# Latent attention with all projections first, two heads a unit, and paired row and column tiles

## What is computed

```python
def mla_project(h, w_down, q_norm_g, kv_norm_g, w_uq, w_ukv, rope):
    cq, ckv, k_rope = jnp.split(h @ w_down, [MLA_Q_RANK, MLA_Q_RANK + MLA_KV_RANK], axis=-1)   # 256, 128, 32
    q = (rms_norm(cq, q_norm_g) @ w_uq).reshape(b, s, MLA_HEADS, MLA_NOPE_DIM + MLA_ROPE_DIM)     # 16 heads, 64 + 32
    q_nope, q_rope = jnp.split(q, [MLA_NOPE_DIM], axis=-1)
    kv = (rms_norm(ckv, kv_norm_g) @ w_ukv).reshape(b, s, MLA_HEADS, MLA_NOPE_DIM + MLA_V_DIM)    # 64 + 64
    k_nope, v = jnp.split(kv, [MLA_NOPE_DIM], axis=-1)
...
def mla_attend(q_nope, q_rope, k_nope, k_rope, v):
    s = (jnp.einsum("bqhd,bkhd->bhqk", q_nope, k_nope)
         + jnp.einsum("bqhr,bkr->bhqk", q_rope, k_rope)).astype(jnp.float32) * (96 ** -0.5)
    p = jax.nn.softmax(s, axis=-1)
    return jnp.einsum("bhqk,bkhe->bqhe", p.astype(v.dtype), v)
```

## Time and profile before

| | us |
|---|---|
| median of 3 runs | 3339.03 |
| lowest, highest | 3336.78, 3340.29 |
| profiled execution | 3339.83 |
| span of its instructions | 3338.5 |
| PE busy in it | 3183.1 (95%) |

### The profile page before, as it was taken

How to read it: one execution, slowest core, us unless ns; L and a number is a source line. 1 busy time by engine, 2 the same in 40 slices (tenths; PEclk the granted TensorE clock), 3 DMA queues, 4 the chain that set the end, 5 groups by cost and what they waited for, 6 DMA issues and landing times.

```text
span 3338.5 us, 51700 instructions
## 1 busy us (share of the span) xinstructions
PE 3183.1 (95%) x21554; PEld 2698.6 (81%) x21554; DVE 1752.5 (52%) x3094; ACT 1404.9 (42%) x2364; POOL 997.9 (30%) x440
## 2 busy tenths in 40 slices
PE   5999999999999998999989999999999999999999
PEld 3777777776677776679989987877999978779999
DVE  3353333555543334666656646555456556654564
ACT  3432222444332223544444445554444446554443
POOL 0312222110212212123433332333444433434433
PEclk8999999999999999999999999999999999999999
DMA  8345544422455552125525542333545433334454
GB/s 290 122 144 164 164 158 133 135 94 89 127 176 167 174 165 90 39 64 182 193 90 164 183 131 81 103 100 98 165 143 188 154 120 99 93 101 152 152 178 151
DMA packets 469303, 460.04 MB, mean 138 GB/s; under 512 B 9040, under 2 KB 467664, under 8 KB 469072
## 3 DMA queue, kind: packets, MB, share of 16 engines
q1 hardware_dynamic: 465760, 453.32, 42.6%
q10 hardware_dynamic: 3312, 3.42, 0.3%
HBM read 455.66 MB, written 1.05 MB: 137 GB/s over the span
## 4 chain that ended last, share of the span: by engine, by line
PE 77%; DVE 13%; ACT 6%; issue 3%; DMA 1%; ACTq 0%; POOL 0%; DVEq 0%
PE bank L399 21%; PE bank L401 20%; PE bank L400 20%; ACT wh L346 3%; DVE wl L362 3%; PE bank L443 3%; DVE hl L760 1%; DVE hidl L760 1%; PE bank L1525 1%; PE bank L1516 1%; PE bank L2258 1%; PE bank L552 1%; DVE tmp L648 1%; PE bank L457 1%; PE bank L1067 1%
## 5 line engine op out<-in xcount | busy, mean ns | idle before, releaser
L374 POOL TENSOR_TENSOR wl<-raw,wh 128x768 fp32r<-128x768 f32 (+1 forms) x336 | 879.8, 2619 | 2159.7 <-ACT wh L346 2149.8
L346 ACT ACTIVATE wh<-raw 128x2048 fp32r<-128x2048 f32 x336 | 636.4, 1894 | 318.4 <-PE bank L401 308.6
L362 DVE TENSOR_TENSOR wl<-raw,wh 128x1280 fp32r<-128x1280 f32 (+1 forms) x336 | 499.6, 1487 | 419.5 <-ACT wh L346 410.6
L399 PE MATMUL bank<-nh,wh 128*128 128x272 f32 (+1 forms) x1712 | 508.1, 297 | 4.5 <-DVE nl L1843 2.8
L401 PE MATMUL bank<-nh,wl 128*128 128x272 f32 (+1 forms) x1712 | 496.1, 290 | 0.0
L400 PE MATMUL bank<-nl,wh 128*128 128x272 f32 (+1 forms) x1712 | 494.5, 289 | 0.0
L399 PE MATMUL bank<-xh,wh 128*128 128x512 f32 (+2 forms) x1264 | 443.0, 350 | 7.8 <-DVE xl L655 5.2
L400 PE MATMUL bank<-xl,wh 128*128 128x512 f32 (+2 forms) x1264 | 432.1, 342 | 0.0
L401 PE MATMUL bank<-xh,wl 128*128 128x512 f32 (+2 forms) x1264 | 431.5, 341 | 0.0
L399 PE MATMUL bank<-hh,wh 128*128 128x512 f32 (+1 forms) x1024 | 350.3, 342 | 3.7 <-DVE X L668 1.9
L399 PEld LDWEIGHTS bank<-nh,wh 128*128 128x128 f32 x1712 | 328.4, 192 | 21.2 <-issue 17.7
(11 more groups left out here) (427 smaller groups left out, 5749.2 us busy)
## 6 DMA issues: line engine op xcount, KB each, us to landing
raw<-in_mlp_w SPq DMA_DIRECT2D x128, 1024.0 KB, 5.3
raw<-in_mod_w SPq DMA_DIRECT2D x83, 1024.0 KB, 5.2
raw<-in_w_in SPq DMA_DIRECT2D x60, 1024.0 KB, 5.2
raw<-in_w_mlp_up SPq DMA_DIRECT2D x32, 1024.0 KB, 5.4
raw<-in_w_mlp_down SPq DMA_DIRECT2D x32, 1024.0 KB, 5.2
raw<-in_w_in SPq DMA_DIRECT2D x34, 512.0 KB, 4.6
raw<-in_w_ssd_down SPq DMA_DIRECT2D x16, 1024.0 KB, 5.2
early<-in_mod_w SPq DMA_DIRECT2D x13, 1024.0 KB, 12.0
```

Source lines behind the costliest of these rows:

```text
L346: nc.scalar.activation(self.wtile(self.wh, c1), self.rawtile(c1), AF.Copy).then_inc(*up("act_wh", ("wh", c1)))
L362: nc.vector.tensor_tensor(l, r, h.bitcast(F32), ALU.subtract).then_inc(*up("dve_wl", ("wl_dve", c1)))
L374: nc.gpsimd.tensor_tensor(l, r, h.bitcast(F32), ALU.subtract).then_inc(*up("pool_wl", ("wl_pool", c1)))
L399: nc.tensor.matmul(o, ah, bh, start=first, stop=False)
```

## The change

- The stream of weights is reordered: the chunk with ckv and k_rope is first, then cq, both halves of keys and values, both halves of queries. DVE's share of the split of the four middle chunks goes from 5/8 to 2/8. The raw tile of a late chunk is the one used longest ago, not number modulo three.
- The columns of w_uq and w_ukv are sorted on the host: the 64-wide parts of eight heads first, then the rotary or value parts.
- cq is computed for the 256 latent tokens alone. The roots of both norms use `dve_quarter_root`, the nine-step DVE chain of the other norms, on four column tiles of a quarter of the tokens; ACT's logarithm and exponential are gone.
- The rotary key is copied to the four groups of 32 rows by four small matmuls and rotated once on 128 rows (`mKR`, kept in tile `tmp3`).
- All keys and values (`mkn`, `mv`), then all queries (`mqn`: eight tiles of two heads; `mqr`: four tiles of four heads, four rotations) are made before the first score.
- A unit of the attention is two heads by one block of 128 queries, 16 units. The scores are two matmuls of 64 rows of contraction on different row groups (line 1571 of the kernel after) and two of 32 rows (1574), accumulated in the same two banks; units alternate between banks 0, 1 and 2, 3. Values are four pairs of 128x64 by 128 queries (1592) on two column groups, into bank 6 or 7. Division and copy are shared between ACT (1683, 1689) and DVE (1771, 1777), and there are three tiles of exponentials.
- Scores lead transposes by two units and values by three. The first six of eight row blocks of output groups 0 and 1 are put between the last units.

The core of the diff:

```diff
+            w(("down", 1), a["mla_w_down"][0], 0, 8, 256, 160)
             w(("down", 0), a["mla_w_down"][0], 0, 8, 0, 256)
-            w(("down", 1), a["mla_w_down"][0], 0, 8, 256, 160)
             for h in range(2):
-                w(("uq", h), a["mla_w_uq"][0], 0, 2, 768 * h, 768)
-                w(("ukv", h), a["mla_w_ukv"][0], 0, 1, 1024 * h, 1024)
+                w(("ukv", h), a["mla_w_ukv"][0], 0, 1, 1024 * h, 1024, 2)
+            for h in range(2):
+                w(("uq", h), a["mla_w_uq"][0], 0, 2, 768 * h, 768, 2)
             for j in range(4):
                 w(("mwo", j), a["mla_w_o"][0], 0, 8, 256 * j, 256)
...
-                t = d % 2 if self.dense[max(d - 4, 0)] < mods[-1] else d % RAWS
+                t = d % 2 if self.dense[max(d - 4, 0)] < mods[-1] else min(range(RAWS), key=lambda i: last[i])
...
+        c = self.ix["down", 0]
+        hi, lo = self.pe_take(c)
+        os = [self.pe_bank((2 + m,), "md", 2 + m)[:, LAT] for m in range(2)]
+        for k in range(8):
+            for m, o in enumerate(os):
+                cs = slice(128 * m, 128 * m + 128)
+                ins = self.mm3(o, hi[:, k, cs], lo[:, k, cs], XH[:, k, LAT], XL[:, k, LAT], k == 0, k == 7)
+                if k == 7:
+                    ins.then_inc(*up("pe_acc", ("acc", "md", 2 + m), *([("used", c)] if m else [])))
+            if k == 2:
+                self.pe_latent(0)
+        self.pe_spread("mkv", BOTH, (5,))
+        raw, turn = self.pe_bank((6,), "mkraw"), self.pe_bank((7,), "mkturn")
...
+        for i in range(4):
+            nc.tensor.matmul(raw[32 * i:32 * i + 32, :], self.ident[0:32, 0:32], self.mkr[0:32, :], start=True, stop=True)
+        for i in range(4):
+            ins = nc.tensor.matmul(turn[32 * i:32 * i + 32, LAT], self.permm[0:32, 0:32], self.mkr[0:32, LAT], start=True, stop=True)
+        ins.then_inc(*up("pe_rope", ("acc", "mkrep")))
+        self.pe_latent(1)
         for hf in range(2):
...
             c = self.ix["ukv", hf]
...
+            hi, lo = (x[:, 0, :] for x in self.pe_take(c))
+            PE.wait_ge(*at("mch", 0, 0))
+            PE.wait_ge(*at("mcl", 0, 0))
+            for p in range(4):
+                b = self.pe_bank(RING, "mk", 4 * hf + p)
+                hs = slice(128 * p, 128 * p + 128)
+                self.mm3(b[:], hi[:, hs], lo[:, hs], self.ckh[:], self.ckl[:], True, True).then_inc(*up("pe_acc", ("acc", "mk", 4 * hf + p)))
+                b = self.pe_bank(RING, "mv", hf, p)
+                tk = slice(128 * p, 128 * p + 128)
+                self.mm3(b[:], self.ckh[:, tk], self.ckl[:, tk], hi[:, 512:1024], lo[:, 512:1024], True, True
+                         ).then_inc(*up("pe_acc", ("acc", "mv", hf, p), *([("used", c)] if p == 3 else [])))
+            if hf == 0:
+                self.pe_spread("mq", LAT, (5,))
+        for i in range(12):
+            self.pe_mla_query(i)
+        for s in range(19):
+            self.pe_mla_step(s)
+            if s in (16, 17):
+                self.pe_mwo(s - 16, 0, 6)
+        for g in range(8):
+            self.pe_mwo(g, 6 if g < 2 else 0, 8)
...
+    QUERIES = (("r", 0), ("n", 0), ("n", 1), ("r", 1), ("n", 2), ("n", 3), ("r", 2), ("n", 4), ("n", 5), ("r", 3), ("n", 6), ("n", 7))
+
+    def pe_mla_query(self, i):
+
...
+        w, n = self.QUERIES[i]
+        c = self.ix["uq", i // 6]
+        hi, lo = self.pe_take(c)
...
+        b = self.pe_bank(RING, "mq", w, n)
+        for k in range(2):
+            H, L = self.mcq[k]
...
+            ins = self.mm3(b[:, LAT], hi[:, k, cs], lo[:, k, cs], H, L, k == 0, k == 1)
+        ins.then_inc(*up("pe_acc", ("acc", "mq", w, n), *([("used", c)] if i % 6 == 5 else [])))
+        if w == "n" and n % 2:
+            self.pe_rope(("m", n // 2), self.mQR[:, n // 2, :], 256, self.permm[:], (7,))
...
+    def pe_mla_step(self, s):
...
+        if s < 16:
+            p, q = s // 2, s % 2
+            qs = slice(128 * q, 128 * q + 128)
+            bs = [self.pe_bank((2 * q + i,), "ms", s, i) for i in range(2)]
+            PE.wait_ge(*at("mqn", p))
+            PE.wait_ge(*at("mkn", p))
+            PE.wait_ge(*at("turned", "m", p // 2))
+            PE.wait_ge(*at("mkturned"))
+            PE.wait_ge(*at("mkcopied"))
+            for i, b in enumerate(bs):
+                r = slice(64 * i, 64 * i + 64)
+                nc.tensor.matmul(b[:], self.mQN[r, p, qs], self.mKN[r, p, :], start=True, stop=False)
+            for i, b in enumerate(bs):
+                r = slice(32 * ((2 * p + i) % 4), 32 * ((2 * p + i) % 4) + 32)
+                nc.tensor.matmul(b[:], self.mQR[r, p // 2, qs], self.mKR[r, :], start=False, stop=True).then_inc(*up("pe_scores", ("acc", "ms", s, i)))
+        u = s - 2
+        if 0 <= u < 16:
+            for i in range(2):
+                b = self.pe_bank((4 + i,), "mt", u, i)
+                PE.wait_ge(*at("mp", u, i))
+                for t in range(4):
+                    ins = nc.tensor.transpose(b[:, 128 * t:128 * t + 128], self.mE[u % 3][:, i, 128 * t:128 * t + 128], self.ident[:])
+                ins.then_inc(*up("pe_turned", ("acc", "mt", u, i)))
+        u = s - 3
+        if 0 <= u < 16:
+            p, q = u // 2, u % 2
+            b = self.place["mo", p] if q else self.pe_bank((6 + p % 2,), "mo", p)
+            PE.wait_ge(*at("mv", p // 4, 3))
+            for i in range(2):
+                PE.wait_ge(*at("mpt", u, i))
+            for t in range(4):
+                for i in range(2):
+                    ins = nc.tensor.matmul(b[64 * i:64 * i + 64, 128 * q:128 * q + 128], self.mV[:, t, 128 * p + 64 * i:128 * p + 64 * i + 64],
+                                           self.mPT[u % 2][:, 4 * i + t, :], start=(t == 0), stop=(t == 3))
+            ins.then_inc(*up("pe_values", ("acc", "mo", u)))
...
+        for i in range(12):
+            self.act_mla_query(i)
+        self.act_split(self.ix["uq", 0])
+        self.act_split(self.ix["uq", 1])
+        for s in range(19):
+            self.act_mla_step(s)
...
+        for n in range(4):
+            self.dve_rope(("m", n), self.mQR[:, n, :], slice(0, 128), 256, cos, sin, self.tmp[n % 3])
+        self.dve_split(self.ix["uq", 0])
+        self.dve_split(self.ix["uq", 1])
+        for s in range(19):
+            self.dve_mla_step(s)
```

More of the change, by code:

```diff
@@ new lines, in pe_mla, with pe_latent @@
+        for i in range(12):
[6 more added lines that the diff above has]
+            self.pe_mwo(g, 6 if g < 2 else 0, 8)
+    def pe_latent(self, u):
+        nc, at, up, PE = self.nc, self.T.at, self.T.up, self.PE
+        keys, T, g, dim, parts = self.latent(u)
+        name = ("mkv", "mq")[u]
+        b = self.pe_bank((4,), "tot", name)
+        for n in range(len(keys)):
+            PE.wait_ge(*at("msq", u, n))
+            for rows, ts, w in self.quarters(T):
+                ins = nc.tensor.matmul(b[rows, 0:w], self.ones[:, 0:32], self.tmp[u + n][:, ts], start=(n == 0), stop=(n == len(keys) - 1))
+        ins.then_inc(*up("pe_acc", ("acc", "tot", name)))
@@ L1561, in act_mla @@
-        rs, rtt, rv = self.mroot
-        ACT.wait_ge(*at("mvar", 1))
-        nc.scalar.activation(rtt[:], rv[:], AF.Ln).then_inc(*ACT.step())
-        ACT.wait_ge(*ACT.now())
-        nc.scalar.activation(rs[:], rtt[:], AF.Exp, scale=-0.5).then_inc(*up("act_root", ("mroot",)))
-        for k in range(3):
-            H = self.cqh[:, k, :] if k < 2 else self.ckh[:]
-            ACT.wait_ge(*at("mct", k))
-            nc.scalar.activation(H, self.tmp[k][:], AF.Copy).then_inc(*up("act_mch", ("mch", k)))
@@ new lines, in act_mla @@
+        for hf in range(2):
+            for p in range(4):
+                ACT.wait_ge(*at("acc", "mk", 4 * hf + p))
+                nc.scalar.activation(self.mKN[:, 4 * hf + p, :], self.place["mk", 4 * hf + p][:], AF.Copy
+                                     ).then_inc(*up("act_out", ("mkn", 4 * hf + p), ("out", "mk", 4 * hf + p)))
+                if p == 3:
+                    self.act_mv(hf, 3)
+            self.act_split(self.ix["ukv", hf])
+            if hf == 0:
+                self.act_latent_high(1)
@@ L1625, in dve_mla @@
-        rs, rtt, rv = self.mroot
-        for u, (name, ks, dim) in enumerate(self.LATENT):
-            DVE.wait_ge(*at("acc", "mtot", u))
-            nc.vector.tensor_scalar(rv[:, 512 * u:512 * u + 512], self.place["mtot", u][:], 1.0 / dim, 1e-6, ALU.mult, ALU.add
-                                    ).then_inc(*up("dve_var", ("mvar", u), ("out", "mtot", u)))
-        DVE.wait_ge(*at("mroot"))
-        nc.vector.tensor_tensor(rtt[:], rs[:], rs[:], ALU.mult).then_inc(*DVE.step())
-        DVE.wait_ge(*DVE.now())
@@ L1642, in dve_mla @@
[L1642 to L1648 removed]
+        self.dve_quarter_root("mkv", BOTH, 128)
@@ new lines, in dve_mla @@
+        self.dve_split(self.ix["down", 1])
+        self.dve_latent(0)
+        raw, turn = self.place["mkraw",], self.place["mkturn",]
+        self.dve_quarter_root("mq", LAT, 256)
+        DVE.wait_ge(*at("acc", "mkrep"))
```

(15 more changed lines are left out.)

370 lines of the change are left out of this document (174 added, 196 removed).

## The result

The changed kernel takes 3304.8 us (median of four, 3301.6 to 3308.3) against 3338.8 before (3336.8 to 3340.3), a ratio of 0.990 with a 95% interval of 0.989 to 0.991: 34 us less, where 41 were forecast. The time lies in the forecast range of 3291 to 3305, but 6.8 us above its middle and only 0.2 us inside its upper edge. The profiled execution of after is the longest of its four, 3308.3 us, so the traces show 31.5 us between the spans.

What follows compares the result with a forecast made beforehand. PE, busy 95% of the span, was taken as the bound. Terms -5.0, -11.8, -1.7, -12.5, -7.6, -4.3 and +2 sum to -40.9 from 3339.83 us; less 0.8 for the profiled execution, 3298 us, range 3291 to 3305.

Steps and rivals of the forecast that it cites:

- What bounds the kernel: Whole kernel: PE busy for 95% of the span, no other engine above 52%, so only PE time and PE's waits count.
- Down-projection: End of the down-projection: cq for 256 tokens instead of 512 makes 48 matmuls cheaper; -5.0 us.
- latents: Between down-projection and PE's next work: serial ACT and DVE chain of 15.1 us shrinks to 3.3; -11.8 us.
- queries: Query matmuls and rotations before the attention: 11.7 us against 24.2; -12.5 us, bounds -13.5 and -10.
- `mwo`: After the attention: 36 matmuls taken from the end and placed between attention work; -4.3 us.
- Keys and values: Key and value matmuls: fewer, but PE waits for DVE's late value copies; 17.6 us against 19.3, -1.7 us.
- second group of waits: Second half of keys and values: PE waits 4.6 us as cq's scaling and low part delay DVE's value copies.
- The start of the attention: First maxima 6.8 us after the last query, PE waiting about 6; fifth unit 9.95 us after the first maxima.
- The clock: Start of the attention: the new 6 us wait brings a stretch at 1.2 GHz; +2 us, 0 to +3.4.
- The unit: Attention, two heads by 128 queries: scores, transposes, values and shape switches take 3.85 us, bounds 3.7 and 4.7.
- Serial tiles: Attention scores: tiles of 32 rows (or the column pairs) don't overlap; 13.7 us more (or 14), 3312; chance 10%.
- The softmax as the bound: Attention: DVE and ACT become the bound, with a period of 4.6 us; 12 us more, 3310; chance 13%.

Runs made afterwards that it cites:

- the leanest unit tried: Changed kernel with the pair of 32-row score matmuls left out of each attention unit; 3281.9 us, a single execution.

## Why the prediction was right, and where it wasn't

- **What bounds the kernel.** Right. PE's waits, PE's time and PE's clock make up every difference found in this stage; in the leanest unit tried PE was still full.
- **Down-projection, latents, queries, `mwo`.** Right within 0.7 us each. The root of ckv did go under cq's matmuls, and the tiles of 32x32 for the rotary key do overlap, four copies by 512 columns in 0.88 us, where one such float32 matmul alone was priced at 0.855; all the latents took 3.6 us:

```profile
1316.38 1.06 PE L1497 MATMUL bank<-mkr,ident 32*32 32x512 f32 x8
1317.26 0.61 PE L1499 MATMUL bank<-mkr,permm 32*32 32x256 f32 x8
```

- **Keys and values.** Right in its sum (18.2 for 17.6) by errors that cancel. The second group of waits was put at 4.6 us and was 1.8. Of these 2.8 us 1.7 are the duration of POOL's split, put at 4.7 us and measured at 3.03; the rest stays open. It was scaled up from 3.15 us, of which some 1.3 had been waiting for DVE. The trace of before had a row with POOL alone, which I hadn't read:

```profile
1412.44 1.89 POOL L374 TENSOR_TENSOR wl<-raw,wh 128x768 fp32r<-128x768 f32 x1 [7.26 <-ACT wh L346]
```

  At that rate 1152 columns are 2.8 us. Against it stood a first wait of 2.1 us instead of 1.5, the clock's 1.7, which I had not foreseen in this stage, and about 1 us for the spreading (0.8 for 0.5) and the slower first matmuls behind waits.
- **The start of the attention.** Right: 16.75 us to the fifth unit without the clock, 17.0 in the run with the wait filled. But behind the third unit the pace was right by luck. The prediction had the chain of DVE and ACT set it, 3.15 us a unit, with PE waiting; the third and fourth unit's scores do stand 3.14 us apart there and in the run with late splits, but PE has no wait between them: two pairs and the transposes, still without values, take it just as long.
- **The clock** was the first step that failed, in its size. I took 2 us, at most 3.4, from a stretch of before with a wait of 5.5 us and 6.8 us at 1.2 GHz. The row was misread as well: the 6.8 us don't follow the wait, half of them lie in it, so that at most 1.7 us of PE's time could be lost by that row. The wait ends at 850.0:

```profile
846.70:850.00 3.30, 0.00 (x0) 0.50 1.06 366
850.00:853.30 3.30, 3.29 (x22) 0.50 1.10 350
```

  Here the stretch was 17.1 us, 13.5 of them behind the wait, and cost 6.3. One such stretch was foretold and there were two, the other the 3.4 us among the keys and values. I had also set part of it off against the chain of DVE and ACT, but with PE at half speed the units (5.9 and 7.7 us apart) were longer than that chain: nothing was hidden. In other executions it was of another length (6.8 to 20.5 us in the six other experiments in which the splits stayed ahead), and the two runs of the changed kernel at 3301.6 and 3302.0 have a mean clock of 0.988 over the span instead of 0.985 and 0.986, which doesn't say in which stretch.
- **The unit** was the second, 4.16 us for 3.85. From the fifth unit to the end it is 60.9 us instead of 56.2, 4.7 more: 3.8 in twelve units, and 0.9 in the transposes, values and `mwo` blocks behind them, where the shapes change as well. The step is "0.96 + 0.96 + 0.93 + 0.97", with some 0.1 for a change of shape. (The values' part calls the four records of the earlier trace rows two pairs; they are one. Its 0.9 us is right for one.) The earlier trace rows read 1.05 for the 64-row pair, which is 0.2 over one matmul; I wrote that down and then took 0.96. It measured 1.06, and each other phase carries 0.15. The Trainium skill, TensorEngine Tiling (Array Packing), Key Properties, by which a change of the tiling mode drains the engine, was the rule to give weight to; one change more cost 0.153 us here. By the Trainium skill, TensorE: Matmul & The Clock Gate, Measured speedup vs the span model, the estimate for the 32-row pair was 1.11 us. It took 1.06, but by the run with both on the same rows it overlaps wholly, and what it has above 0.855 is the change.
- **The rivals.** Serial tiles would have cost 13.7 us; when forced they cost 0.853 us a unit, 13.6 in sixteen. The softmax as the bound, to which I gave 13%, was never near. With the measured size of these two terms in its place, the sum on the profiled execution would have been 3298.9 + 4.3 + 4.7 = 3307.9; that execution took 3308.3. That it comes so close is in part luck, as the errors of the other terms cancel.

Not settled: why the stretch at 1.2 GHz differs so much in length after the same wait, and why PE begins the second head's values before the first head's are done, but not at once.

## What to carry to other kernels

A wait of PE costs more than its length: here 5.4 us of it, of which 4.4 could go, brought 6.3 us of lower clock on top, so weight splits that aren't needed yet belong inside the stretch in which PE has work queued, not ahead of it. When tiles of different shapes are mixed, count the changes of shape (0.15 to 0.2 us each here) as carefully as the matmuls. Never scale the duration of a DVE or POOL operation in SBUF from a row in which the other engine ran beside it; look for one where it was alone.
